# The softmax scaling of the prompt's attention: from VectorE to GpSimd, in one queue with the value-page loads

## The reference, cut to what matters

```python
def sparse_attend(q, k_sel, v_sel, valid):
    s = jnp.einsum('bthd,btkhd->bthk', q, k_sel).astype(jnp.float32) * (HEAD_DIM ** -0.5)
    s = jnp.where(valid[:, :, None, :], s, -jnp.inf)
    p = jax.nn.softmax(s, axis=-1).astype(v_sel.dtype)
    return jnp.einsum('bthk,btkhd->bthd', p, v_sel)
```

## Time and profile before

| | |
|---|---|
| median of three runs | 1591.12 us (1590.04 to 1594.01) |
| the profiled execution's own time | 1593.75 us |
| its span, first to last instruction | 1592.1 us |
| PE busy | 1495.8 us, 94% |
| DVE busy | 1043.9 us, 66% |
| ACT busy | 519.7 us, 33% |
| POOL busy | 487.2 us, 31% |
| the stage 768.2 to 1104.3 us: PE, DVE, ACT, POOL busy | 291.83, 256.37, 179.05, 69.87 us |

### The profile page before, as it was taken

One profiled execution on the slowest core, in us unless ns is written; L12 is line 12 of the kernel. 1 busy time (PEld: TensorE's weight loads), 2 busy tenths in 40 slices (PEclk: granted clock), 3 DMA queues, 4 the chain that ended last, 5 costly groups with the idle time before them and its releaser, 6 DMA issues.

```text
span 1592.1 us, 30573 instructions
## 1 busy us (share of the span) xinstructions
PE 1495.8 (94%) x11418; PEld 1371.1 (86%) x11418; DVE 1043.9 (66%) x1708; ACT 519.7 (33%) x991; POOL 487.2 (31%) x454
## 2 busy tenths in 40 slices
PE   5999999999999999999888888888899999999999
PEld 4988988999999999999656666566888898998998
DVE  5447654599999999900587778775985657009332
ACT  5335455212233001020355555553103602334111
POOL 6321243235523323233112222221563244133110
PEclk9999999999999999999999999999999999999999
DMA  6021233022232323210676667766015543213111
GB/s 221 3 77 42 75 88 95 30 93 86 95 134 108 103 96 108 67 56 2 223 242 199 195 235 251 235 210 214 22 52 158 167 149 118 85 59 108 45 37 34
DMA packets 116756, 183.77 MB, mean 115 GB/s; under 512 B 23105, under 2 KB 76162, under 8 KB 116610
## 3 DMA queue, kind: packets, MB, share of 16 engines
q1 hardware_dynamic: 104834, 146.69, 27.7%
q0 software_dynamic: 11776, 35.14, 6.9%
HBM read 147.95 MB, written 33.83 MB: 114 GB/s over the span
## 4 chain that ended last, share of the span: by engine, by line
PE 81%; DVE 9%; ACT 3%; issue 3%; DMA 1%; SPq 1%; POOL 1%; ACTq 0%; DVEq 0%; POOLq 0%
PE PS L1058 27%; PE PS L1462 13%; PE PS L1129 7%; PE PS L1065 6%; PE PS L1099 4%; PE PS L1324 3%; PE PS L1233 2%; PE PS L1261 2%; PE PS L1252 2%; PE PS L1305 2%; PE PS L1269 2%; ACT buf L1724 1%; PE PS L1281 1%; PE PS L1292 1%; DVE buf L1989 1%
## 5 line engine op out<-in xcount | busy, mean ns | idle before, releaser
L1933 DVE TENSOR_SCALAR_CACHE_REDUCE buf<-buf,buf 128x384 f32<-128x384 f32 (+6 forms) x224 | 243.4, 1152 | 1.1
L1058 PE MATMUL PS<-hn_lo,w_hi 128*128 128x384 f32 x720 | 234.9, 326 | 0.0
L1058 PE MATMUL PS<-hn_hi,w_lo 128*128 128x384 f32 x720 | 234.8, 326 | 0.0
L1058 PE MATMUL PS<-hn_hi,w_hi 128*128 128x384 f32 x720 | 234.7, 326 | 0.0
L888 POOL CAST w_hi<-buf 128x2048 fp32r<-128x2048 f32 (+2 forms) x43 | 74.4, 1731 | 466.1 <-DMA buf<-in_w_in_dram 146.2
L889 POOL TENSOR_TENSOR w_lo<-buf,w_hi 128x2048 fp32r<-128x2048 f32 (+2 forms) x43 | 180.9, 4207 | 3.5
L1462 PE MATMUL PS<-w_hi,mix_hi 128*128 128x256 f32 (+1 forms) x576 | 164.6, 286 | 2.7 <-DVE mix_lo L2117 2.7
L1462 PE MATMUL PS<-w_lo,mix_hi 128*128 128x256 f32 (+1 forms) x576 | 162.9, 283 | 0.0
L1462 PE MATMUL PS<-w_hi,mix_lo 128*128 128x256 f32 (+1 forms) x576 | 162.8, 283 | 0.0
L661 POOL DMA_DIRECT2D buf<-in_cache_v_dram x128 | 69.9, 546 | 286.0 <-PE PS L1305 174.6
L1724 ACT ACTIVATE buf<-PS 128x512 f32<-128x512 f32 (+4 forms) x200 | 101.5, 508 | 136.4 <-PE PS L1261 88.8
(11 more groups left out here) (281 smaller groups left out, 3510.9 us busy)
## 6 DMA issues: line engine op xcount, KB each, us to landing
buf<-in_cache_k_dram SPq DMA_DIRECT2D x128, 256.0 KB, 4.2
buf<-in_cache_v_dram POOLq DMA_DIRECT2D x128, 256.0 KB, 4.5
buf<-in_w_in_dram SPq DMA_DIRECT2D x26, 1024.0 KB, 6.0
gates_scratch<-buf SPq DMA_DIRECT2D x40, 544.0 KB, 2.9
buf<-gates_scratch SPq DMA_DIRECT2D x40, 544.0 KB, 4.4
buf<-in_x_prompt_dram SPq DMA_DIRECT2D x16, 512.0 KB, 4.5
out_dram<-buf SPq DMA_DIRECT2D x34, 128.0 KB, 1.7
out_dram<-buf SPq DMA_DIRECT2D x2, 2048.0 KB, 7.7
```

Of the source, the lines that this page charges most:

```text
L1058: last = mm(ps[0:min(w, P), 512 * j:512 * j + tn], wt[:, k, P * half:min(w, P * half + P)], xt_[:, k, t0:t0 + tn], start=m == 0, stop=m == ...
L1933: run(V.tensor_scalar(marks[j][0:r], v, t, None, op, ALU.add, accum_out=CN[0:r, j:j + 1]), ch, wait=j == NJ - 1)
```

## The change

The reciprocal stays on DVE and now counts a new semaphore, `att_inverse`. The multiplication moves to POOL. POOL walks through `plan` too: at an N it waits for the reciprocal and multiplies; at K0.7 it issues the first 14 loads of value pages; at a V it issues the loads up to 14 pages past what that V uses. So the loads and the multiplications share one queue, in the order of `plan`. Two semaphores become one (`omlb_ready` is counted on `lb_diff`), and an unused tile of 4 words (`mx`) is dropped, by which the tiles behind it move by 16 bytes.

```diff
-        mx, nm, rsum, rinv = [xf(4) for _ in range(4)]
+        nm, rsum, rinv = [xf(4) for _ in range(3)]
...
             pool.wait_ge(sem("topk_bias"), NJ)
-            pool.wait_ge(sem("ring2_full"), ring_no["K", 0, 7] + 1)
-            for n in range(BS * NPG):
-                if n >= NVP:
-                    pool.wait_ge(sem("vpage_used"), n - NVP + 1)
-                page_load(pool, vpage[n % NVP], cv, n // NPG, n % NPG, sem(f"vpage_load{n % NVP // 2}"))
+            nv = 0
+
+            def v_pages(m):
+
+                nonlocal nv
+                for n in range(nv, min(m, BS * NPG)):
+                    if n >= NVP:
+                        pool.wait_ge(sem("vpage_used"), n - NVP + 1)
+                    page_load(pool, vpage[n % NVP], cv, n // NPG, n % NPG, sem(f"vpage_load{n % NVP // 2}"))
+                nv = max(nv, m)
+            for kind, b, x in plan:
+                if kind == "N":
+                    pool.wait_ge(sem("att_inverse"), b + 1)
+                    p_ = Pp[b % NPP][:, 0:P * (att_steps[b][0] + 1)]
+                    run(nc.gpsimd.tensor_scalar(p_, p_, rinv[:, b % 4:b % 4 + 1], None, ALU.mult), sem("att_normed"))
+                elif (kind, b, x) == ("K", 0, 7):
+                    pool.wait_ge(sem("ring2_full"), ring_no["K", 0, 7] + 1)
+                    v_pages(NVP)
+                elif kind == "V":
+                    v_pages(NVP + b * NPG + min(4 * x + 4, NPG))
...
-            act.wait_ge(sem("omlb_ready"), 1)
+            act.wait_ge(sem("lb_diff"), 2)
...
-            run(V.tensor_scalar(omlb, lb, -1.0, 1.0, ALU.mult, ALU.add), sem("omlb_ready"))
+            run(V.tensor_scalar(omlb, lb, -1.0, 1.0, ALU.mult, ALU.add), sem("lb_diff"))
...
                 elif kind == "N":
-                    nk, q = P * (att_steps[b][0] + 1), b % 4
+                    q = b % 4
                     dve.wait_ge(sem("att_exp"), b + 1)
-                    run(V.reciprocal(rinv[:, q:q + 1], rsum[:, q:q + 1]), ch)
-                    p_ = Pp[b % NPP][:, 0:nk]
-                    run(V.tensor_scalar(p_, p_, rinv[:, q:q + 1], None, ALU.mult), sem("att_normed"))
+                    run(V.reciprocal(rinv[:, q:q + 1], rsum[:, q:q + 1]), sem("att_inverse"))
```

## The result

The changed kernel took 1613.05 us (median of 4 runs, 1612.06 to 1616.21) against 1592.57 us of the kernel before on the same chip: ratio 1.0118, 95% interval 1.0086 to 1.0150. A second set of runs (after2) gave 1613.92 us against 1592.62 us, ratio 1.0128 (1.0102 to 1.0155). The forecast was 1596.6 us with a range up to 1601: the sign is right, the size is not; 5.5 us were expected and some 20 came. The profiled execution took 1616.21 us, the longest of the four; its span is 1614.3 us against 1592.1 us.

A forecast was written before the change was run, and what follows sets the result against it. PE was taken to bound the kernel (81% of the chain). Stop 3.3, N4 0.2 and clock 2.0 us summed to 5.5 us on the median of 1591.1 us: 1596.6 us, range 1590.5 to 1601 us.

The forecast's parts named there:

- DVE loses 64 multiplications: DVE's queue: some 33 us leave, only N2 and N3 on the path, worth 0.6 us, swallowed by the stop.
- The stop at T2: First rounds: N2 waits on POOL behind 14 loads, PE stops 4.6 us at T2; S0.3 comes 3.3 us later.
- POOL gains 64 multiplications: POOL's price for 1024 columns: taken as a cast's 1.04 us, upper bound 2.39 us from a two-input operation.
- N4: Multiplication ahead of T4, the one tight place: 0.2 us counted, from 0 to 1.7.
- POOL's queue, later groups: Seven later groups: N8 and N12 end 2.3 us before T8 and T12 need them; no cost at either bound.
- the point of decision: Later groups: above 3.3 us for 1024 columns each group would pay too, and the time would pass 1601 us.
- The clock: PE's work after the stop: a low-clock stretch is likely, costing 2.0 us, bounds 0 and 2.6 us.
- The rest: Two semaphores made one and tiles shifted by 16 bytes: 0, from -0.5 to +0.5 us.
- POOL's multiplication is dear: Rival: at 2.39 us a piece the loads start later and N4 costs 1.5 us more: 1598.7 us; chance 0.13.

The follow-up runs named there:

- copy: Changed kernel with GpSimd copying each row of probabilities onto itself in place of the multiplication (scaling left out), same queue order: 1599.22 us, ratio 1.0028.
- spload: Changed kernel with value pages loaded from SP's queue, POOL doing only the multiplications at 2.85 us for 1024 columns: 1594.99 us, ratio 1.0004.
- with price and order mended: Changed kernel with a copy in place of the multiplication, and 4 of the first 14 loads at K0.7, 10 behind N3: 1596.04 us, ratio 1.0005.
- tt: Changed kernel with the multiplication written as a product of two tiles, the second the reciprocal repeated along the row, same queue order: 1595.76 us, single run.
- after: The changed kernel itself, against the kernel before: 1613.05 us, ratio 1.0118.
- imm: Changed kernel with the multiplication by the constant 0.5 in place of the scalar per partition: 1608.54 us, single run.

## Why the prediction was wrong

- *DVE loses 64 multiplications: 0.6 us at most, swallowed.* Right. DVE is 35 us less busy, and the run without them is at 1.0002.
- *The stop at T2.* Right in place and cause, and right in size for the operation assumed (4.34 us with a copy). With the real one, N0 and N1 take 5.8 us and not 2.1, so the 14 loads begin at 783.95 us and not at 783.11, N2 itself takes 0.6 us and not 0.3, and PE comes to T2 at 794.29 us and not at 794.70: 6.1 us.
- *POOL gains 64 multiplications; I take the cast.* This step failed. The operation takes 2.85 us and the cast 1.04. I chose by the number of tiles read, and took a product of two tiles as the upper end; neither bounds it. N4 then cost 2.4 us and not 0.2. The sentence of the Trainium skill (GPSIMD Engine Reference, section Key points: about twice VectorE) gave an estimate of 1.5 us; the trace does not agree, 2.85 us is 3.8 times DVE's 0.75 us.
- *POOL's queue, later groups: nothing, at either bound.* This step failed too, and it is the larger part of the miss: nothing was forecast, and the six groups have 6.9 us more of idle (4.4 in the second profile) and 2 to 3 us more of PE busy. I took the times of the last loads ahead of N8 and N12 from the trace of before (821.16 and 842.29 us), as if the loads stayed where they were, and I counted four loads ahead of a pair; between N11 and N12 there are eight. The four multiplications N8 to N11 now stand ahead of these in the same queue and push them back. I asked whether the loads would be late for PE, and not whether they would hold up the next pair. By that working the point of decision was 3.3 us a row; the runs place it between 1.90 us, where the groups are as before, and 2.85 us.
- *The clock: 2.0 us.* Right for one stop (2.2 us in the copy's run). With two stops there were two more low stretches in the first rounds, at 797.2 and 810.9 us, and 4.2 us more of PE busy; 7.0 us in the whole stage (6.4 in the second profile). How much of that the change brings is open: spload, with as little idle as the kernel before, has 4.0 us more of PE busy in the stage at ratio 1.0004.
- *The rest: 0.* Nothing in the stage is left for it: with price and order mended, its 335.2 us come back. The 2.8 us behind the stage lie within what equal work scatters there.

Of the rivals, "POOL's multiplication is dear" was the nearest, with 0.13; it too left out the queue, by which each group pays at 2.85 us already, below its line of 3.3 us, and so its price of 1598.7 us fell short.

## What to carry to other kernels

An operation that the trace does not show on the new engine has no upper bound in another operation of that engine, however like it seems; let the range say so. When work is put into a queue that issues transfers, write the new queue out in order with durations, moved work and transfers alike, and let every entry push the next; the times of the old trace hold for none of them. And ask first what the relieved engine's time is worth: here a run of the kernel without the multiplications would have shown that there was nothing to gain.

## What the runs showed of the hardware

On POOL a multiplication of one f32 tile by a scalar took longer than a product of two tiles: 2.85 us for 1024 columns against 2.54 us for 1088. From 128 to 1024 columns a copy goes from 295 to 1042 ns (copy), 0.83 ns a column; a product with a repeated second operand from 404 to 1898 ns (tt), 1.67 ns a column; the multiplication by a scalar from 606 to 2851 ns (after), 2.51 ns a column: as one to two to three. A constant in place of the scalar per partition saves 0.07 us, no more (imm). On this queue, in the changed kernel, the first load behind a multiplication begins 1.21 us after it, where the next begins 0.61 us after the one before.
